# Conv layer of a two-layer decoder step: taps inside the next block, another order on VectorE, sixteen last taps, three output blocks chunk by chunk

## The reference

```python
mod = einsum('bd,lde->lbe', silu(c), w_ada) + b_ada          # 2 layers x 6 x 1024 rows, 9 conditions
h = rmsnorm(x, g) * (1 + scale_m) + shift_m
a, gate = split(h @ w_in, 2)                                 # 1024 -> 2 x 1024
u = a * sigmoid(gate)
u = causal_depthwise_conv(u, state, w_dw, b_dw)              # width 31
u = layernorm(u, ln_g, ln_b)
y = silu(u) @ w_out
x = x + gate_m * rmsnorm(y, g_post)
```

## Time and profile before

| | |
|---|---|
| runs | 1600.32, 1602.41, 1603.86 us |
| the profiled execution | 1602.89 us, of it the span from first to last instruction 1601.3 us |
| TensorE busy | 1517.7 us (95%) |
| weight loads of TensorE | 1372.6 us (86%) |
| VectorE busy | 1013.1 us (63%) |
| ScalarE busy | 880.4 us (55%) |
| mean DMA rate | 171 GB/s |

### The profile page before, as it was taken

One profiled execution on the slowest core, in us unless ns is written; L12 is line 12 of the kernel. 1 busy time (PEld: TensorE's weight loads), 2 busy tenths in 40 slices (PEclk: granted clock), 3 DMA queues, 4 the chain that ended last, 5 costly groups with the idle time before them and its releaser, 6 DMA issues.

```text
span 1601.3 us, 28430 instructions
## 1 busy us (share of the span) xinstructions
PE 1517.7 (95%) x11350; PEld 1372.6 (86%) x11350; DVE 1013.1 (63%) x1530; ACT 880.4 (55%) x1628; POOL 138.5 (9%) x364
## 2 busy tenths in 40 slices
PE   5999988999999999999999988999999999999997
PEld 4676654899999999999978866667999999999997
DVE  4599986479764498654725434665588664577743
ACT  4554556668663486643614544665577653566632
POOL 1000000000000033200000011110000000133200
PEclk9999999999999999999999989999999999999998
DMA  9665555425455445454426335664235555354552
GB/s 367 235 220 211 211 188 188 163 72 169 169 181 177 142 147 171 161 202 143 145 70 238 120 125 204 218 223 166 86 105 172 169 184 172 125 180 161 185 178 97
DMA packets 71765, 273.77 MB, mean 171 GB/s; under 512 B 8032, under 2 KB 10096, under 8 KB 71120
## 3 DMA queue, kind: packets, MB, share of 16 engines
q1 hardware_dynamic: 65248, 246.44, 44.5%
q0 software_dynamic: 6096, 25.15, 4.7%
q10 hardware_dynamic: 288, 0.35, 0.1%
HBM read 262.80 MB, written 8.85 MB: 170 GB/s over the span
## 4 chain that ended last, share of the span: by engine, by line
PE 79%; DVE 10%; ACT 5%; issue 4%; DMA 2%; SPq 0%; DVEq 0%; ACTq 0%
PE ps L650 57%; PE ps L627 3%; PE ps L873 3%; PE ps L717 3%; DVE odd_taps L1692 2%; ACT w_hi L1120 2%; DVE w_lo L1523 2%; PE ps L926 2%; PE ps L932 1%; PE ps L909 1%; DVE y L1692 1%; PE ps L993 1%; PE ps L945 1%; DVE y L1789 1%; PE ps L960 1%
## 5 line engine op out<-in xcount | busy, mean ns | idle before, releaser
L650 PE MATMUL ps<-h_hi,w_hi 128*128 128x288 f32 x1920 | 572.8, 298 | 15.6 <-DVE w_lo L1523 13.8
L1523 DVE TENSOR_TENSOR w_lo<-raw,w_hi 128x1024 fp32r<-128x1024 f32 (+1 forms) x309 | 403.1, 1306 | 266.3 <-ACT w_hi L1120 266.2
L650 PE MATMUL ps<-h_lo,w_hi 128*128 128x288 f32 x1920 | 566.4, 295 | 0.0
L650 PE MATMUL ps<-h_hi,w_lo 128*128 128x288 f32 x1920 | 566.3, 295 | 0.0
L1120 ACT ACTIVATE w_hi<-raw 128x1024 fp32r<-128x1024 f32 (+1 forms) x309 | 346.9, 1123 | 108.3 <-PE ps L650 73.3
L650 PEld LDWEIGHTS ps<-h_hi,w_hi 128*128 128x128 f32 x1920 | 361.0, 188 | 23.1 <-DVE w_lo L1523 17.9
L650 PEld LDWEIGHTS ps<-h_lo,w_hi 128*128 128x128 f32 x1920 | 361.1, 188 | 0.9
L650 PEld LDWEIGHTS ps<-h_hi,w_lo 128*128 128x128 f32 x1920 | 361.0, 188 | 0.0
L650 PE MATMUL ps<-act_hi,w_hi 128*128 128x288 f32 x704 | 208.3, 296 | 0.0
L650 PE MATMUL ps<-act_lo,w_hi 128*128 128x288 f32 x704 | 207.7, 295 | 0.0
L650 PE MATMUL ps<-act_hi,w_lo 128*128 128x288 f32 x704 | 207.0, 294 | 0.0
(11 more groups left out here) (241 smaller groups left out, 1989.5 us busy)
## 6 DMA issues: line engine op xcount, KB each, us to landing
raw<-w_k_dram SPq DMA_DIRECT2D x245, 512.0 KB, 3.5
raw<-w_down_dram SPq DMA_DIRECT2D x64, 704.0 KB, 4.0
ada_w<-w_ada_dram SPq DMA_DIRECT2D x76, 512.0 KB, 5.4
k_page<-cache_kt_dram SPq DMA_DIRECT2D x32, 512.0 KB, 5.1
v_page<-cache_v_dram POOLq DMA_DIRECT2D x32, 512.0 KB, 5.1
ada_h<-w_ada_dram SPq DMA_DIRECT2D x8, 512.0 KB, 7.0
ada_u<-w_ada_dram SPq DMA_DIRECT2D x6, 512.0 KB, 15.6
x<-x_in_dram SPq DMA_DIRECT2D x1, 2304.0 KB, 10.7
```

The costliest lines, as they stand in the source:

```text
L650: mm = pe.matmul(ps[:, BANK[b], 0:HALF], lhsT=w[s][:, kb * P:(kb + 1) * P], rhs=v[:, at, :] if down else v[:, at, lo:hi], start=(at == 0 a ...
L1523: dve.tensor_tensor(w_lo[s][:, 0:cols], raw[n % RING][:, 0:cols], w_hi[s][:, 0:cols].bitcast(F32), ALU.subtract).then_inc(s_lo, 1)
```

## The change

1. Input stage: the pieces and the transpose of quarter q + 2 now stand behind the q-th chunk product, so two quarters are read before chunk 4 and chunk 1; weight 1 is split earlier; the low part of the new tokens comes ahead of the second chunk's product.
2. Input loop on TensorE: from block 4 on, the taps stand in the middle of the even block, behind four of its eight chunks.
3. Input loop on VectorE: `EARLY_TAPS` says how many of a chunk's steps come before the next gate product: all 26 of chunk 0, then 18, 18, 18, 18, 18, 6, 0 of the others; four of them come ahead of a split, three late ones behind the gate product. `TURNS_FROM` is the first step that goes to the second tile; steps before it are in place. It is also the step that takes in TensorE's sum. The first gate product comes ahead of its splits.
4. TensorE takes 7 taps of chunk 6 and 16 of chunk 7. A diagonal tile holds 7, `diag_more` holds 9 and takes the place of the eighth own tile of the pieces; `c_raw` moves to temporary space.
5. The 16 taps stand behind four late pieces. Seven own pieces follow them, then seven mean sums and five pieces. Then each of the four squares of half 0 stands ahead of one piece.
6. Blocks 16, 17 and 18 consume half 0 chunk by chunk; then four pieces, block 19 and the last four pieces.
7. Half 1's silu, rounding and low parts are moved from ahead of the output blocks' drains to between them (`SILU_AT`). A weight in slots 3 to 5 no longer waits for all pieces.

The diff, cut to its core:

```diff
-PE_TAPS = [6] * (C - 1) + [12]
+PE_TAPS = [6] * (C - 2) + [7, 16]
+DIAG_TILE = 7
+EARLY_TAPS = [WA - PE_TAPS[0] + 1] + [18] * (C - 3) + [6, 0]
+TURNS_FROM = [9] + [1] * (C - 2) + [3]
-OWN_TILE = range(LATE_PIECES + ADA_RING, LATE_PIECES + ADA_RING + 8)
+OWN_TILE = range(LATE_PIECES + ADA_RING, LATE_PIECES + ADA_RING + 7)
+SILU_AT = {0: (0, 1), 1: (2, 3), 2: (4,), 3: (5,), 4: (6,), 5: (7,), 6: (8,)}
...
 # TensorE
-            for q in range(QUARTERS):
-                if q < QUARTERS - 1:
-                    first_pieces(q + 1)
-                    first_turn(q + 1)
-                for kb in FIRST_CHUNKS[2 * q:2 * q + 2]:
...
+            first_pieces(1)
+            first_turn(1)
+            for n, kb in enumerate(FIRST_CHUNKS):
+                pe.wait_ge(h_ready, (STEP[0, kb, None] if n % 2 else STEP[0, kb, 1]) + 1)
+                both_halves(0, kbs=(kb,))
+                both_halves(1, kbs=(kb,))
+                if n + 2 < QUARTERS:
+                    first_pieces(n + 2)
+                    first_turn(n + 2)
...
-                if b % 2 == 0:
+                if b % 2:
+                    both_halves(b)
+                else:
+                    part = C // 2 if b > 2 else 0
+                    both_halves(b, range(part))
                     conv_taps(b // 2 - 1)
-                both_halves(b)
+                    both_halves(b, range(part, C))
...
-            late_pieces(ADA_RING + len(OWN_TILE))
+            late_pieces(ADA_RING)
+            conv_taps(C - 1)
+            late_pieces(len(OWN_TILE))
             for n in range(C - 1):
                 mean_sum(n)
-            late_pieces(4)
+            late_pieces(PIECES - ADA_RING - len(OWN_TILE))
             mean_sum(C - 1)
-            late_pieces(4)
             for p in range(C // 2):
                 square_sum(0, p)
+                late_pieces(1)
             square_sum(1, 0)
             late_pieces(4)
...
             for kb in range(C):
                 norm_wait(1, kb, 0)
-                one_half(b, kbs=(kb,))
-                one_half(b + 1, kbs=(kb,))
+                for b in range(2 * C, 2 * C + RING):
+                    one_half(b, kbs=(kb,))
                 if kb in (1, 3, 5):
                     square_sum(1, (kb + 1) // 2)
-            late_pieces(PIECES * GROUPS - piece)
+            late_pieces(4)
...
                 next_block(b)
+                if b == 2 * C + 3:
+                    late_pieces(PIECES * GROUPS - piece)
 # ScalarE
                     if BLOCKS[LOAD_FIRST[n]].phase == "a_out":
                         act.wait_ge(conv_stored, 32)
-                        act.wait_ge(ada_done, PIECES * GROUPS)
+                        if SLOT[n] > RING + 2:
+                            act.wait_ge(ada_done, PIECES * GROUPS)
...
             for b in range(2 * C, Q1):
                 after_block(b)
+                for n in SILU_AT.get(b - 2 * C, ()):
+                    ln_silu(n, 1)
                 if b == 2 * C + 3:
                     copy_group(GROUPS - 1)
 # VectorE
+            glu(0)
+            split_ahead(0)
+            split_ahead(1)
+            for i in range(1, C):
+                early, made = EARLY_TAPS[i - 1], WA - PE_TAPS[i - 1] + 1
+                ahead = early if i == 1 else min(early, 4)
+                early_taps(i - 1, range(0, ahead))
                 split_ahead(2 * i)
+                early_taps(i - 1, range(ahead, early))
...
                 glu(i)
+                late = min(made - early, 3)
+                late_taps(i - 1, range(early, early + late))
                 if i < C - 1:
                     split_ahead(2 * i + 1)
+                late_taps(i - 1, range(early + late, made))
+                seq_conv(i - 1)
...
             for b in range(2 * C, Q1):
                 after_block(b)
+                for n in SILU_AT.get(b - 2 * C, ()):
+                    if n < C:
+                        norm_make(1, n, 1)
+                    if n >= 2:
+                        norm_low(1, n - 2, 1)
+                    if n == C:
+                        norm_low(1, C - 1, 1)
```

More of the change, by code:

```diff
@@ L361, in trunk_kernel @@
                    for j in range(len(OWN_TILE))]
-        diag = [place(f"diag{s}", [P, PE_TAPS[0], P], at=at) for s in range(2)]
-        diag_more = place("diag_more", [P, PE_TAPS[-1] - PE_TAPS[0], P], at=[h_off + 8 * C * P * 4, h_off + 9 * C * P * 4])
+        diag = [place(f"diag{s}", [P, DIAG_TILE, P], at=at) for s in range(2)]
+        diag_more = place("diag_more", [P, PE_TAPS[-1] - DIAG_TILE, P], at=[h_off + 7 * C * P * 4, h_off + 9 * C * P * 4])
         k_t = place("k_t", [P, PAIRS, TT], at=(at := wide()))
@@ L379, in trunk_kernel @@
         h_first = place("h_first", [P, 2, TP], at=temp())
+        c_raw = place("c_raw", [P, C, NB], at=temp())
         sq = place("sq", [P, 2, TT], at=temp(4 * HALF * 4))
@@ L847, in up_pair @@
                 chain_stats(b + 1)
-            for b in range(2 * C + 2, V0):
+            for b in range(2 * C + RING, V0):
                 if b in (UP0, UP0 + 1):
@@ L1186, in _ @@
             split(0)
+            split(1)
             act.wait_ge(a_stat, 1)
@@ L1225, in _ @@
                     act.wait_ge(taps_pe, i - 1)
-                for k in range(PE_TAPS[0]):
+                for k in range(min(PE_TAPS[i], DIAG_TILE)):
                     act.activation(diag[i % 2][:, k, :], ident[:], ACT.Copy, scale=prm("w_a_dw", i * WA + k))\
@@ L1234, in _ @@
                     act.wait_ge(gemm_done, 2 * C)
-                    for k in range(PE_TAPS[0], PE_TAPS[i]):
-                        act.activation(diag_more[:, k - PE_TAPS[0], :], ident[:], ACT.Copy,
+                    for k in range(DIAG_TILE, PE_TAPS[i]):
+                        act.activation(diag_more[:, k - DIAG_TILE, :], ident[:], ACT.Copy,
                                        scale=prm("w_a_dw", i * WA + k)).then_inc(diag_made, 1)
@@ L1260, in ln_scale, with ln_silu @@
                 act.activation(rs[:, lo:hi], rs[:, lo:hi], ACT.Exp, scale=-0.5).then_inc(a_rs, 1)
-            def ln_silu(h):
-                for n in range(C + 1):
-                    if n < C:
-                        silu_step(n, h)
-                    if n:
-                        silu_hi(n - 1, h)
-                    if h == 0 and n in (1, 3, 5):
-                        ln_square(1, (n + 1) // 2)
+            def ln_silu(n, h):
+                if n < C:
+                    silu_step(n, h)
+                if n:
+                    silu_hi(n - 1, h)
             act.preload_act_table_set(LN_EXP)
@@ L1280, in _ @@
             ln_scale(0)
-            ln_silu(0)
+            for n in range(C + 1):
+                ln_silu(n, 0)
+                if n in (1, 3, 5):
+                    ln_square(1, (n + 1) // 2)
             ln_scale(1)
-            ln_silu(1)
             def stat_scale(c, what):
@@ L1677, in tap @@
             def tap(i, n):
-                g, k = TAP_DONE[i - 1] if i else 0, PE_TAPS[i] + n
-                if g + n:
-                    dve.wait_ge(taps, g + max(n - 1, 0))
-                whole = y[:, i, 0:TP]
-                out = odd_taps[:] if n % 2 else whole
+                g, k, turn = TAP_DONE[i - 1] if i else 0, PE_TAPS[i] + n, TURNS_FROM[i]
+                whole, odd = y[:, i, 0:TP], n >= turn and (n - turn) % 2 == 0
+                out = odd_taps[:] if odd else whole
                 if k == WA:
                     dve.wait_ge(taps, g + n)
-                    ins = dve.tensor_tensor(whole, whole, odd_taps[:], ALU.add)
-                elif n == 0:
+                    dve.tensor_tensor(whole, whole, odd_taps[:], ALU.add).then_inc(taps, 1)
+                    return
+                last = n - 1 if n <= turn and not odd else n - 2
+                if n == 0 or n == turn:
+                    if g:
+                        dve.wait_ge(taps, g)
+                else:
+                    dve.wait_ge(taps, g + max(last, 0) + 1)
+                if n == 0:
                     ins = dve.tensor_scalar(out, u_p[:, i, k:k + TP], prm("w_a_dw", i * WA + k), prm("b_a_dw", i),
@@ L1689, in tap, with early_taps, late_taps @@
                 else:
-                    if n == 1:
+                    if n == turn:
                         dve.wait_ge(taps_pe, i + 1)
                     ins = dve.scalar_tensor_tensor(out=out, in0=u_p[:, i, k:k + TP], scalar=prm("w_a_dw", i * WA + k),
-                                                   in1=ps[:, 4 + i % 2, :] if n == 1 else out,
+                                                   in1=ps[:, 4 + i % 2, :] if n == turn else out,
                                                    op0=ALU.mult, op1=ALU.add)
                 ins.then_inc(taps, 1)
-            early = (WA - PE_TAPS[0]) // 2
-            def early_taps(i):
-                dve.wait_ge(pair_free[1], i + 1)
-                for n in range(early):
+            def early_taps(i, part):
+                if part.start == 0:
```

(17 more changed lines are left out.)

28 lines of the change are left out of this document (8 added, 20 removed).

## The result

The changed kernel takes 1608.64 us (median of 5 runs, 1605.35 to 1609.57), the kernel before 1602.41. The ratio is 1.0036, with a 95% interval of 1.0021 to 1.0051: slower by about 6 us, where I had forecast 1598.0 and a range that ended at 1604. The profiled run took 1609.08 us with a span of 1607.5; before it was 1601.3.

A forecast was written before the change was run, and what follows sets the result against it. TensorE and VectorE were taken as both nearly full in the input loop. Terms 4.4 + 3.7 + 3.0 - 0.1 - 0.8 - 5.0 - 0.8 gave 4.4 us, so 1598.0 against 1602.4; own range 1596 to 1600.5, with rivals 1593.5 to 1604.

The forecast's parts named there:

- Input stage, 4.4 us: Block 0's taps start at 49.5 instead of 53.93: 2.3 from earlier modulation pieces, 2.1 from the freed gate product.
- Loop and chunk 6, 6.7 us: Input loop: 3.7 us gained from vanished tap waits, 3.0 at chunk 6's seven taps with the clock held.
- the sum at block 15's end: Gains of input stage, loop and chunk 6 together: 11.1 us at the end of block 15.
- Rival (d): Input loop gains nothing because VectorE with its moved steps is as late as before: 1601.7 us, chance 0.08.
- rival (a): Clock falls at waits before the seven or sixteen taps, each costing 2.95 us: 1601.0 for one, chance 0.22.
- Last taps to first chunk, −0.1 with bounds of 3: Block 15's end to first output chunk takes 48.2 us, before 48.1: nothing gained, bounds -3 and +3.
- What this adds (1.3 us) the squares take back: Before the first output chunk, 1.3 us added ahead of the mean is regained, as squares no longer follow four transfer-paced pieces.
- fifth ring piece: Ahead of the last mean: this piece waits for its transfer and ends about 2.9 us after the fourth.
- Output blocks, −5.8 us: Three blocks chunk by chunk lose 0.8 us in the chunk stage and 5.0 for block 19's weight and ScalarE's rounds.
- ScalarE's rounds not binding: Rival for blocks 19 to 24: TensorE runs on its own work, gain 8.4 us, time 1594, chance 0.13.
- The clock, −0.8: Half of a 1.7 us low-clock loss, taken as possible after the 3.1 us idle before the last transpose.
- (c): Output blocks: ScalarE's rounds are longer than 5 us; at 7 us the time is 1607, chance 0.12.

The follow-up runs named there:

- e11: e7 with the edits of the input stage undone: 1592.9 us, ratio 0.9939 against the kernel before.
- e2: Changed kernel with the four late pieces again in one run ahead of the squares: 1601.8 us, ratio 1.0000 against the kernel before.
- e3: Changed kernel with the edits of e1 and e2 together: 1593.3 us, ratio 0.9953 against the kernel before.
- e1: Changed kernel with the old output stage put back: 1598.4 us, ratio 0.9980 against the kernel before.
- e6: e3 with the four pieces moved behind the squares, so eight follow in one run: 1601.7 us, ratio 1.0002 against the kernel before.
- e7: e3 with fifteen last taps instead of sixteen and eight pieces in tiles of their own: 1589.5 us, ratio 0.9932 against the kernel before.
- e8: e2 with the weights of blocks 19 to 21 issued ahead of the last four pieces: 1593.1 us, ratio 0.9950 against the kernel before.
- e10: e9 with VectorE's products for half 1 one round earlier: 1583.8 us, ratio 0.9891 against the kernel before.
- e9: The edits of e7 and e8 together: 1591.6 us, ratio 0.9923 against the kernel before.
- e5: Changed kernel with filler matmuls added, 20 behind the fourth ring piece and 18 behind the last mean: 1609.1 us, ratio 1.0055 against the kernel before.

## Why the prediction was wrong, by its steps

- **Input stage, 4.4 us.** 2.8 at block 0's taps. I had freed the gate product from a split, and not asked what is late next: ScalarE's diagonals. By the end of the loop e11 shows 4.2, with 3 us of scatter between equal fronts, and the time of e11 shows 1 us. So how much of the 4.4 was won stays open.
- **Loop and chunk 6, 6.7 us.** Right within a microsecond in this profile: the sum at block 15's end is 10.2 against 11.1 forecast. Rival (d) falls, and rival (a) at the seven taps. At the sixteen taps (a) came true in part: they did wait about 2 us as forecast, and the clock fell over the first seven of them (7.94 us against 6.25 in e2 and e3), 1.7 us that the sum had not counted.
- **Last taps to first chunk, −0.1 with bounds of 3: here it failed.** It cost 8.9 us: 2.3 ahead of the last mean, where 1.3 was forecast, and 6.6 behind it, where a gain of 1.3 was. The failed sentence is "What this adds (1.3 us) the squares take back". I took the pieces between the last mean and the squares for an obstacle on TensorE's path. They were what it did while ScalarE and VectorE made the first squares. Taking them out of there saves almost nothing, since the first square is made no sooner (245.06 against 245.28 in e3), and they come back later at full price or, standing singly, at twice their price: from the last mean on, e2 shows 6.4 us, e3 against e1 8.1, e6 against e3 7.1. The fifth ring piece, which I did price, was 2.5 us together with the sixteenth tap (e7).
- **Output blocks, −5.8 us.** B grew by 6.0 us against before, and by 7.9 in e2 against e3. Place and size were right. (The start of the pieces, 264.5, is 0.25 early by the prediction's own terms, which changes nothing.) The division was not: with ScalarE's rounds not binding I had the gain at 8.4 instead of 5.2, so 3.2 us for the rounds and 1.8 for the weight. e8 took 9.9 us from B by the weights' place in SyncE's queue alone, and the rounds were 2.5 us (e10 against e9, B).
- **The clock, −0.8.** Too small. It stood at 0.50 for 10.2 us twice. What that cost is in A and B; in A it was 2.8 us by e5, and 1.7 at the last taps. (The page's slices of the kernel before never show it under 0.8; half clock stands only in short stretches as those of the earlier trace rows, so the slices alone don't warn of it.)
- **The sum** with measured terms: 10.2 − 8.9 − 6.0 − 1.5 = −6.2 us, the difference of the two spans.

My rival for a slower kernel, (c), looked at ScalarE's rounds; they came 4.8 and 5.1 us apart, as in the forecast. The mechanism that made it slower was one that I had booked at a gain of 1.3 us. The bounds of 3 us on that stretch had no row behind them.

Not settled is why the front of equal kernels differs by up to 3 us between profiled runs (block 15's end from 205.0 in the changed kernel to 208.1 in e1), why the same 2.03 us wait ahead of the last taps was followed by the low clock in some kernels and not in others, and what the 1.5 us behind the last transpose are.

## What to carry to other kernels

Before work is moved off the path, look at what the engine would do in the time it leaves: filler that stands in a wait for other engines is free only there. In the two other places tried here it cost its own time, its transfers and some of the clock. When a step is moved past a queue, list what stands behind it in that queue: one weight behind four pieces on SyncE made TensorE wait 9.2 us, and issuing the weights of three blocks ahead of those pieces took 9.9 us from B. A term that is booked at zero needs a row for its cover just as a cost needs one for its size.

## What was not expected of the hardware

- The clock: after TensorE had been busy for 1.72 us in the 4.4 us from 236.2, the granted clock stood at 0.50 for 10.2 us, in which it worked 8.09 us. In e3 a similar gap (2.78 us) was followed by 3.5 us at 0.52, with TensorE busy for 3.16 of them. The extra work in e5 kept it at 1.00 throughout.
- The same wait of 2.03 us ahead of the last taps was followed by seven taps in 7.94 or 7.95 us in the changed kernel, e1, e5, e6 and e8, and in 6.25 us in e2 and e3, whose instructions up to there are the same.
- A modulation piece (4 records of 128*32, 128x512) takes 1.05 us alone and 1.92 us in a run of four (16 records), both at the full clock.
- Matmuls of 128x128 as filler took 0.12 us per record (40 in 4.73 us), each call leaving two records. I had reckoned one record for a call.
